# Three instead of four adaLN conditioning units in each normalisation gap, and two idle TensorE products behind them, in a four-layer decoder step

## The reference

```python
mod = jax.nn.silu(c) @ w + b                      # adaLN: (sequences, 6*1024)
sh1, sc1, g1, sh2, sc2, g2 = split(mod, 6)
h = rms_norm(x, g) * (1 + scale) + shift          # before each sub-layer
x = x + gate * sub_layer(h)                       # after it
```

## Time and profile before

| | |
|---|---|
| median of 3 runs | 2364.89 us (2361.26 to 2372.58) |
| the profiled execution, its own time | 2360.04 us |
| its span from the first to the last instruction | 2358.2 us |
| mean granted TensorE clock over the span | 0.926 of full speed |
| TensorE busy | 2077.8 us, 88% |
| VectorE, ScalarE busy | 1139.7 us and 806.4 us |
| HBM traffic of the span | 191 GB/s read and written |

### The profile page before, as it was taken

One profiled execution on the slowest core, in us unless ns is written; L12 is line 12 of the kernel. 1 busy time (PEld: TensorE's weight loads), 2 busy tenths in 40 slices (PEclk: granted clock), 3 DMA queues, 4 the chain that ended last, 5 costly groups with the idle time before them and its releaser, 6 DMA issues.

```text
span 2358.2 us, 34057 instructions
## 1 busy us (share of the span) xinstructions
PE 2077.8 (88%) x13538; PEld 1757.6 (75%) x13538; DVE 1139.7 (48%) x1918; ACT 806.4 (34%) x1468; POOL 31.4 (1%) x57
## 2 busy tenths in 40 slices
PE   3897999999986556999978999997899999889997
PEld 1784999989964434799956999743577777669997
DVE  2463653479353223654467544576434434345532
ACT  1311443245332112443224432333333333324522
POOL 0000000000000000000000000000000000000000
PEclk8898999999978777999989999996799999889999
DMA  6775555643424557665655656530035645624442
GB/s 250 252 250 194 192 202 202 231 143 126 129 81 121 161 161 230 214 203 206 232 193 179 203 208 207 202 105 17 23 116 183 210 155 168 201 91 143 151 154 76
DMA packets 229499, 398.67 MB, mean 169 GB/s; under 512 B 9288, under 2 KB 195567, under 8 KB 215793
## 3 DMA queue, kind: packets, MB, share of 16 engines
q1 hardware_dynamic: 224912, 332.69, 42.7%
q0 software_dynamic: 3296, 59.76, 7.7%
q10 hardware_dynamic: 1161, 4.34, 0.5%
HBM read 391.23 MB, written 59.76 MB: 191 GB/s over the span
## 4 chain that ended last, share of the span: by engine, by line
PE 79%; DVE 8%; DMA 6%; ACT 3%; issue 2%; SPq 1%; ACTq 0%; POOL 0%; DVEq 0%; POOLq 0%
PE bank L1117 36%; PE bank L1023 10%; PE bank L1594 8%; PE bank L988 4%; PE bank L1036 4%; PE bank L1092 3%; DMA work<-in_state_swa 3%; DVE rstd L1813 2%; PE bank L1204 2%; PE bank L1401 2%; PE bank L1603 1%; PE bank L1346 1%; DMA work<-in_ada_w 1%; PE bank L1605 1%; SPq L498 1%
## 5 line engine op out<-in xcount | busy, mean ns | idle before, releaser
L1680 DVE TENSOR_TENSOR ring_lo<-ring,ring_hi 128x1024 fp32r<-128x1024 f32 (+1 forms) x324 | 380.0, 1213 | 365.6 <-ACT ring_hi L681 365.5
L681 ACT ACTIVATE ring_hi<-ring 128x1024 fp32r<-128x1024 f32 (+1 forms) x324 | 323.1, 1046 | 333.6 <-PE bank L1117 279.6
L1117 PE MATMUL bank<-hidden_hi,ring_hi 128*128 128x320 f32 x1024 | 318.9, 311 | 0.0
L1117 PE MATMUL bank<-hidden_hi,ring_lo 128*128 128x320 f32 x1024 | 316.4, 309 | 0.0
L1117 PE MATMUL bank<-hidden_lo,ring_hi 128*128 128x320 f32 x1024 | 316.3, 309 | 0.0
L1117 PE MATMUL bank<-h_hi,ring_hi 128*128 128x320 f32 x896 | 279.6, 312 | 0.1
L1117 PE MATMUL bank<-h_lo,ring_hi 128*128 128x320 f32 x896 | 276.2, 308 | 0.0
L1117 PE MATMUL bank<-h_hi,ring_lo 128*128 128x320 f32 x896 | 275.9, 308 | 0.0
L988 PE MATMUL bank<-tab,work 128*128 128x128 f32 (+6 forms) x708 | 141.4, 331 | 147.7 <-DMA work<-in_state_swa 75.2
L988 PEld LDWEIGHTS bank<-tab,work 128*128 128x128 f32 (+6 forms) x708 | 89.3, 161 | 189.8 <-DMA work<-in_state_swa 77.0
L1117 PEld LDWEIGHTS bank<-hidden_hi,ring_hi 128*128 128x128 f32 x1024 | 192.2, 188 | 20.1 <-issue 20.1
(11 more groups left out here) (263 smaller groups left out, 3379.6 us busy)
## 6 DMA issues: line engine op xcount, KB each, us to landing
ring<-in_mlp_w SPq DMA_DIRECT2D x128, 1024.0 KB, 5.5
work<-in_ada_w SPq DMA_DIRECT2D x88, 1024.0 KB, 7.5
ring<-in_swa_w_qkv SPq DMA_DIRECT2D x18, 1024.0 KB, 5.0
out_swa_s<-in_state_swa POOLq DMA_DIRECT2D x8, 2016.0 KB, 10.0
ring<-in_conv_w_in SPq DMA_DIRECT2D x12, 1024.0 KB, 6.2
work<-in_state_swa SPq DMA_DIRECT2D x48, 256.0 KB, 10.0
work<-in_cache_mla SPq DMA_DIRECT2D x64, 160.0 KB, 2.2
ring<-in_ada_w SPq DMA_DIRECT2D x8, 1024.0 KB, 11.8
```

Source lines behind the costliest of these rows:

```text
L681: act.activation(ring_hi[:, place, part], ring[:, s, part], ACT.Copy).then_inc(sem("weights_hi"), 1)
L1117: mm = pe.matmul(bank[a % 4][:, 0:T], w[:, k, :], x(k), start=first and k == 0 and j == 0, stop=last and k == KD - 1 and j == 2)
L1680: dve.tensor_tensor(ring_lo[:, s, part], ring[:, s, part], ring_hi[:, place, part], ALU.subtract)\
```

## The change

Each of the six gaps of layers 1 to 3 has three conditioning units instead of four (units 0 to 2 and 21 to 23), and the MLP between has 18 instead of 16 (units 3 to 20): behind the even units of the MLP, and behind its units 7 and 23 as well. The loads are reordered to match. Behind the conditioning units of gaps 1 to 7 stand two products of the matrix of ones with 512 columns of the tables, into bank 7, whose result nobody reads.

```diff
-GAP_SIDES = 4
+GAP_SIDES = 3
 GAP_FIRST = 1
+GAP_WARM = 2
+SIDE_BEHIND = sorted([*range(0, 32, 2), 7, 23])
...
-                    if sides and u in (1, 3):
+                    if sides and u in (0, 2):
                         load_side(sides, SIDE_LAYER - 2 + u // 2)
...
-                elif u >= RING and u % 2 == 0:
-                    load_side(l + 1, GAP_SIDES + u // 2)
-                if u in (29, 31):
-                    load_side(l + 1, SIDE_LAYER - GAP_SIDES + (u - 29) // 2)
+                if u - RING in SIDE_BEHIND:
+                    load_side(l + 1, GAP_SIDES + SIDE + SIDE_BEHIND.index(u - RING))
...
-            plain("mla_kva", A["mla_w_kva"][0], 2)
+            plain("mla_kva", A["mla_w_kva"][0], 1)
             load_side(3, SIDE_LAYER - 1)
+            plain("mla_kva", A["mla_w_kva"][0], 2, first=1)
...
                 for s in gap[GAP_FIRST:]:
                     side_unit(*s)
+                for _ in range(GAP_WARM if ni else 0):
+                    pe.matmul(bank[7][:, :], ones, tab[:, 0:512], start=True, stop=True)
...
-                    if l + 1 < DEPTH and u % 2 == 0:
-                        side_unit(l + 1, GAP_SIDES + u // 2)
+                    if l + 1 < DEPTH and u in SIDE_BEHIND:
+                        side_unit(l + 1, GAP_SIDES + SIDE_BEHIND.index(u))
```

More of the change, by code:

```diff
@@ L418, in load_side, with plain @@
                   .then_inc(sem(f"side_landed{v % SIDE}"), 16)
-            def plain(phase, w, n, kc=KD, cols=256, col0=0, sides=None):
+            def plain(phase, w, n, kc=KD, cols=256, col0=0, sides=None, first=0):
                 v = w.rearrange("(k p) n -> p k n", p=P)
-                for u in range(n):
+                for u in range(first, n):
                     U = UNIT0[phase] + u
```

## The result

| | before | changed |
|---|---|---|
| median of 20 runs each, us | 2364.65 (2356.69 to 2372.58) | 2375.6 (2368.61 to 2378.8) |
| ratio, 95% interval | | 1.0042 [1.0033, 1.0052] |
| the profiled execution, us | 2360.04 | 2377.35 |
| its span, us, and mean granted clock | 2358.2, 0.926 | 2375.5, 0.923 |

The changed kernel is 9.9 us slower (0.0042 x 2364.65). The time lies in the range that was given and still within 0.5%, but the forecast was 3.5 us.

A forecast was written before the change was run, and what follows sets the result against it. TensorE was taken as the bound, with 79% of the chain that ended last. The terms 7.1 - 3.1 - 0.5 = +3.5 us made 2360.04 into 2363.5, or 2368 us on the median; the range was 2360 to 2377.

The forecast's parts named there:

- the price of the moved units: Six units moved behind MLP products cost 1.18 us each, uncovered because TensorE never waits there: +7.1 us.
- the idle products' own price and their cover: Two take 2.05 us at full clock, 4.1 at half, and cost nothing where they end before block 0 of `h_lo`.
- the rival in which they delay the first products: Idle products at half clock take 4.1 us and end after block 0 of `h_lo`: +14.0, 2379 us; chance 0.10.
- the loads: Unit 23's load lands in time, 482.7 at the latest against 483.6 needed; no conditioning-load wait in gaps 2, 4 and 6.
- all 14.2 us of those waits would be gained: Rival: all conditioning-load waits were on the path and vanish with the half clock: -13.6, 2351 us; chance 0.05.
- Gap 6 gave 0.5 as said: In gap 6 the products ahead of ScalarE's first result end earlier, bounded by block 1 of `h_lo`: -0.5 us.
- gaps 4 and 7: Forecast 0 in both; at best 0.9 us gained in gap 4 and 1.1 in gap 7 at full clock.
- gap 3: Forecast 0, taken between a gain of 1.7 us and a loss of 0.5 from idle products at half rate.
- the return of gap 2: Without the late unit, 87 products behind gap 2 run at full clock, 13.02 us instead of 16.26, ending earlier: -3.1 us.
- the 0 for gaps 1 and 5: The 87 products there already run at full clock, so no change; at worst that clock falls, 3.2 us each.
- the prediction's own sign of being wrong: Profile signs against it: `in_ada_w` among longer waits, `h_lo` ready before idle products end, granted clock 0.50 behind gaps 1 or 5.
- the late load and the lost clock of gap 2 together: Unit 23 still lands late, or gap 2's clock is lost; a late load leaves only +7.1, 2372 us; joint chance 0.10.

The follow-up runs named there:

- e4: The changed kernel with two units in each gap instead of three, twelve moved instead of six, loads to match: 2387.72 us, ratio 1.0083.
- e1: The changed kernel without the idle products, the six units still moved: 2378.06 us, ratio 1.0048.
- e3: The changed kernel plus one idle product of 320 columns behind block 0's nine products in gaps 1, 2, 3, 5 and 6: 2368.12 us, ratio 1.0019.
- e6: The changed kernel with three idle products in each gap instead of two: 2367.78 us, ratio 1.0019.
- e7: The kernel before, unaltered, run once more for a second profile: 2368.73 us, one execution.
- e2: The kernel before, no unit moved, with two idle products behind the four units of each gap: 2371.18 us, ratio 1.0022.
- e5: The kernel before with one unit moved out of gap 2, two idle products there and a 320-column one between blocks in gaps 2 and 5: 2362.85 us, 0.9998.
- e8: The changed kernel, unaltered, run once more for a second profile: 2374.25 us, one execution.

## Why the prediction was off by 6 us

**Right: the price of the moved units.** 1.18 us for each of six, 7.1; the MLPs grew by 7.2, and by 14.3 with twelve units moved (e4).

**Right: the idle products' own price and their cover.** 2.05 us at full clock against 1.98 and 1.99 in gaps 1 and 2; they end before `h_lo` in those gaps and nobody waits for them. In gap 5 of the first execution they ended as block 0 came, and the wait for block 1 covered that. So the rival in which they delay the first products did not occur in the changed kernel, and e1 excludes it as the cause of the loss.

**Right: the loads.** No `work` load is waited for any more, unit 23 comes in time. That all 14.2 us of those waits would be gained did not happen: `h_lo` took their place in the list of waits. Gap 6 gave 0.5 as said, gaps 4 and 7 nothing.

**Near by luck: gap 3.** The forecast was 0, between a gain and a loss by idle products at half rate; +0.4 and +0.5 were measured. But the idle products ran at full rate (1.98 us) and ended 2.91 us ahead of block 0. The loss is clock that fell with block 1, as in gaps 1 and 2.

**The step that failed** is the return of gap 2, -3.1, which rested on "That it stays full I take from gap 1, where TensorE idled 2.31 us and its clock held", and with it the 0 for gaps 1 and 5. The 3.1 us were there: e3 and e6 have them. But the changed kernel lost the clock in that gap, and lost it in gap 1 as well, where it had been full. That is the prediction's own sign of being wrong, a granted clock of 0.50 behind gap 1. The comparison with gap 1 took the length of one wait as the measure, and that does not order the cases. Before, a late unit stood in the middle of gap 1's idle time, by accident of its DMA. It split it into 2.31, 0.23 and 1.38 us in the first execution and into 1.33 and 1.35 in e7:

```profile
232.44 1.07 PE L1092 MATMUL bank<-work,silu_c 128*32 128x512 f32 x8 [1.33 <-DMA work<-in_ada_w]
...
236.37 0.41 PE L1036 MATMUL bank<-h_hi,ring_hi 128*128 128x320 f32 x1 [1.35 <-DVE h_lo L1724]
```

The change takes this unit away, puts the idle products directly behind the other units and leaves two waits with nothing between them but block 0's nine products. Behind gap 1 the clock fell in all three profiled executions with three units, at most two idle products behind them and none between the blocks (15.47, 15.56 and 15.59 us), and in none of the four with four units there (13.02, 13.03, 13.02 and 13.03: before, e7, e2, e5). In gap 2, 0.70 us of work in the second wait (e3) or 0.9 more ahead of the first (e6) sufficed to undo it, in one profiled execution each.

That it was the late unit that held the clock is not shown, and gap 5 speaks against it as the whole reason. There the kernel before has no late unit, only two waits of 1.51 and 1.37 us (first line), and its clock held in both executions; the same two waits, a little shorter in sum, lost it in e8 (the other two):

```profile
1262.44 0.41 PE L1036 MATMUL bank<-h_hi,ring_hi 128*128 128x320 f32 x1 [1.37 <-DVE h_lo L1724]
```

```profile
1265.21 0.38 PE L1037 MATMUL bank<-h_hi,ring_hi 128*128 128x320 f32 x1 [1.31 <-DVE h_lo L1727]
...
1268.14 0.64 PE L1037 MATMUL bank<-h_hi,ring_hi 128*128 128x320 f32 x1 [1.38 <-DVE h_lo L1727]
```

So the sum, for the first and the second pair of executions, is 7.2, plus 2.4 and 2.6 in gap 1, minus 0.4 and 1.4 in gap 2, plus 0.4 and 0.5 in gap 3, nothing or 2.6 in gap 5, minus 0.5 and 0.8 in gap 6: 9.1 and 10.7.

The prediction's sentences on the bound had this case in them: 3.2 us for each of gaps 1 and 5 "at worst", and no return in gap 2. It gave them little chance (0.10 for the late load and the lost clock of gap 2 together), and its rivals looked for a clock lost by delay, by idle products at half rate, not for one lost in the waits that are left. The time lies in the range because the range reached up to the price of such a rival, not because the sum was right. The Trainium skill, TensorE: Matmul & The Clock Gate, section Part 1: The HAM clock gate, says that the monitor runs freely, so the moment at which the clock changes moves from run to run. The traces agree: in two executions of one program the clock rose at different points of gap 5's units (3.64 and 2.16 us), and the products behind took 13.02 and 15.67 us.

**What is open.** Why the clock falls behind one pair of waits and not behind another, no run tells. It fell behind 1.56 and 1.37 us in gap 2 of both executions of the change, and behind 1.31 and 1.38 in gap 5 of e8; it held behind 1.51 and 1.37 in gap 5 of the kernel before and behind 1.50 and 1.37 in gap 1 of e4. The lengths of the waits alone do not order these cases. And the medians of e3 and e6, +0.19% or 4.5 us by the ratio, lie somewhat above what their touched places sum to (7.2 - 3.1 - 1.3 - 0.5 = +2.3 for e3), though inside the interval of 0.7 to 8.0 us.

## What to carry to other kernels

Work that stands in a wait is free there and paid in full behind an engine that never waits: before it is moved, the gap must have something to give back that is larger. Idle products that are to hold TensorE's clock must shorten the idle time next to the products that count: two behind the units did not suffice here, a third behind them or a short one between the blocks did. What stands in the idle time already, a late unit too, may be doing part of this job; gap 1 points to it here, gap 5 does not. An edit of a few microseconds is judged by the stages that it touches in two or more executions, since here untouched stages moved by 6 us.

## What the runs showed that was not expected

The clock fell to 0.50 with no single wait above 1.75 us behind gap 1's units in the changed kernel, and none above 1.38 in gap 5 of e8, and held through 2.31 us in gap 1 before. In gaps 1 and 2 it fell only with the second, shorter wait: block 0's nine products still ran at full rate (0.31 us a record), in gap 1 of e1 even behind 3.57 us of idle time, while in gaps 2, 3 and 5 of e1 block 0 was at half rate behind 3.47, 3.17 and 2.75. A unit of 0.96 us costs 1.18 when it stands between products of another shape.
